# Weight-block sums of a two-layer trunk kernel: a fourth block formed in SBUF by adding transfers, and the others spread out

## What is computed

```python
for i in range(DEPTH):                       # DEPTH = 2
    mem_kv = rmsnorm(mem, mem_norm[i]) @ w_mem_kv[i]
    u = rmsnorm(h, norm_mix_pre[i])
    ...                                      # layer 0: Mamba-2 SSD, layer 1: windowed attention with sinks
    mixed = jnp.concatenate([y_mix, y_mem], axis=-1) @ w_out
    h = h + rmsnorm(mixed, norm_mix_post[i])
    f = squared_relu_mlp(rmsnorm(h, norm_mlp_pre[i]), w_up[i], w_down[i])
    h = h + rmsnorm(f, norm_mlp_post[i])

def squared_relu_mlp(u, w_up, w_down):
    return jnp.square(jax.nn.relu(u @ w_up)) @ w_down      # w_up 1024 x 4096, w_down 4096 x 1024
```

## Time and profile before

| what | value |
|---|---|
| runs, median of 3 | 1314.51 us (1312.38, 1314.51, 1319.97) |
| profiled execution | 1316.26 us, its span 1314.5 us |
| TensorE busy | 1288.1 us, 98% of the span |
| VectorE, ScalarE, GpSimd busy | 812.3, 657.4, 162.8 us |
| DMA | 230.01 MB, mean 175 GB/s |
| mean granted TensorE clock | 0.992 |
| chain that ended last | PE 87%, DMA 5%, DVE 4%, ACT 2%, issue 1% |

### The profile page before, as it was taken

The page is one execution under the profiler, slowest core; times in us unless marked ns, Lnnn a source line. Parts: engine busy times, 40 slices in busy tenths (PEclk is TensorE's granted clock), DMA queues, the critical chain, the costliest instruction groups (busy, mean ns, idle before and its releaser), DMA issues.

```text
span 1314.5 us, 17993 instructions
## 1 busy us (share of the span) xinstructions
PE 1288.1 (98%) x6743; PEld 1062.0 (81%) x6743; DVE 812.3 (62%) x1160; ACT 657.4 (50%) x1141; POOL 162.8 (12%) x195
## 2 busy tenths in 40 slices
PE   9999999999978999999999999999999999999998
PEld 8777788888757988888888888777779888888886
DVE  5586686887432733336787973776464334478887
ACT  6644455677332532325555743675453323365563
POOL 0046362551110000000000000000000000000000
PEclk9999999999989999999999999999999999999999
DMA  6378773343977269678656526656534775966654
GB/s 218 105 249 282 194 231 105 121 150 112 251 166 208 80 190 226 207 181 207 205 193 194 189 81 156 130 117 156 137 124 140 183 216 169 222 199 191 193 166 156
DMA packets 110367, 230.01 MB, mean 175 GB/s; under 512 B 8134, under 2 KB 18646, under 8 KB 110038
## 3 DMA queue, kind: packets, MB, share of 16 engines
q1 hardware_dynamic: 84240, 159.93, 36.9%
q0 software_dynamic: 21760, 67.11, 23.2%
q10 hardware_dynamic: 4294, 2.00, 0.9%
HBM read 225.69 MB, written 70.04 MB: 225 GB/s over the span
## 4 chain that ended last, share of the span: by engine, by line
PE 87%; DMA 5%; DVE 4%; ACT 2%; issue 1%; ACTq 0%; DVEq 0%; SPq 0%
PE G L1961 47%; PE G L2390 4%; PE G L2392 4%; PE G L2388 4%; DMA raw<-in_ssd_w_out 3%; PE X L2390 3%; PE X L2388 3%; PE X L2392 3%; PE X L1984 3%; PE X L2042 3%; PE G L2042 2%; PE X L2157 1%; DVE wlo L1275 1%; PE X L2231 1%; PE X L2148 1%
## 5 line engine op out<-in xcount | busy, mean ns | idle before, releaser
L1275 DVE TENSOR_TENSOR wlo<-raw,whi 128x1024 fp32r<-128x1024 f32 x143 | 175.7, 1229 | 297.4 <-ACT whi L693 297.3
L1961 PE MATMUL G<-uhi,whi 128*128 128x512 f32 x736 | 294.4, 400 | 1.0 <-DVE sz L1400 0.6
L1961 PE MATMUL G<-uhi,wlo 128*128 128x512 f32 x736 | 287.1, 390 | 0.0
L1961 PE MATMUL G<-ulo,whi 128*128 128x512 f32 x736 | 286.7, 390 | 0.0
L693 ACT ACTIVATE whi<-raw 128x1024 fp32r<-128x1024 f32 x143 | 151.5, 1059 | 257.5 <-PE G L1961 165.4
L1098 ACT ACTIVATE whi<-raw 128x1024 fp32r<-128x1024 f32 x112 | 118.7, 1059 | 122.0 <-PE G L2392 69.9
L1735 DVE TENSOR_TENSOR wlo<-raw,whi 128x1024 fp32r<-128x1024 f32 x112 | 136.4, 1223 | 65.4 <-ACT whi L1098 65.3
L1961 PEld LDWEIGHTS G<-uhi,whi 128*128 128x128 f32 x736 | 138.2, 188 | 32.3 <-issue 2.3
L1961 PEld LDWEIGHTS G<-uhi,wlo 128*128 128x128 f32 x736 | 138.1, 188 | 29.5 <-DVE wlo L1323 0.2
L1961 PEld LDWEIGHTS G<-ulo,whi 128*128 128x128 f32 x736 | 138.3, 188 | 28.6
L608 POOL DMA_DIRECT2D tsum<-in_w_down x32 | 32.7, 1022 | 559.4 <-PE G L1961 554.7
(11 more groups left out here) (371 smaller groups left out, 2483.3 us busy)
## 6 DMA issues: line engine op xcount, KB each, us to landing
tsum<-in_w_down POOLq DMA_DIRECT2D x48, 1024.0 KB, 10.1
raw<-in_w_up SPq DMA_DIRECT2D x64, 512.0 KB, 4.2
raw<-tsum SPq DMA_DIRECT2D x64, 512.0 KB, 3.8
raw<-in_w_down SPq DMA_DIRECT2D x48, 512.0 KB, 4.2
raw<-in_ssd_w_in SPq DMA_DIRECT2D x20, 512.0 KB, 3.7
raw<-in_w_mem_kv SPq DMA_DIRECT2D x16, 512.0 KB, 3.6
raw<-in_ssd_w_out SPq DMA_DIRECT2D x16, 512.0 KB, 6.3
raw<-in_swa_w_in SPq DMA_DIRECT2D x16, 512.0 KB, 4.3
```

Of the source, the lines that this page charges most:

```text
L1275: dve.tensor_tensor(wlo[q][:, :, :], raw[q % 2][:, :, :], whi[q][:, :, :].bitcast(F32), ALU.subtract).then_inc(lo_done, 1)
L1961: mm = pe.matmul(o, st, mv, start=(kt == 0 and fresh and not go_on), stop=(q == total - 1 and k == 1), skip_group_check=True)
```

## The change

**The fourth block.** `tsum` has three blocks. The 16 transfers per layer that were blocks 2 and 3 become the 8 of block 2. M6's eight panels are now loaded by SP from block 2 into the raw buffers, the same data as M1's. Behind each such load, GpSimd waits for its landing (`down_in`) and issues an accumulating transfer of the 512 KB panel of `w_down` onto the raw buffer in SBUF (`last_add`, landing counted by the new semaphores `full_in`). ACT's `right_hi` waits for `full_in` in M6 where it waited for `down_in`.

**The others.** The 16 copies of blocks 0 and 1 now begin with three at panels 2, 4 and 6 (`COPY_AT`), and the rest go two per SSD unit, which leaves room for three adds in units 6 and 7. The remaining 13 transfers for layer 0 wait for panels 54, 57, 60 and then for every second one from 72 to 90. For layer 1 there are 16, at every second panel from 162 to 174 and from 190 to 206.

**The boundary behind layer 0's MLP** (odd `m`) has another order on ACT and DVE, for token tiles 2 and 3.

```diff
-WEIGHT_SUM = {M2: (0, (5, 11)), M1: (2, (8, 14)), M7: (1, (6, 12)), M6: (3, (10, 16))}
-W0_SUM_AT = tuple(range(54, 64)) + tuple(range(72, 100, 2))
-W1_SUM_AT = tuple(range(162, 184, 2)) + tuple(range(190, 216, 2))
+WEIGHT_SUM = {M2: (0, (5, 9)), M1: (2, (8, 12)), M7: (1, (6, 10)), M6: (2, (8, 12))}
+COPY_AT = (2, 4, 6)
+W0_SUM_AT = (54, 57, 60) + tuple(range(72, 92, 2))
+W1_SUM_AT = tuple(range(162, 176, 2)) + tuple(range(190, 208, 2))
...
+            def last_add(i, q):
+
+                n = 8 * M6 + q
+                src = a["w_down"][i][2048:4096, 512:1024][256 * q:256 * q + 256, :].rearrange("(k p) n -> p k n", p=P)
+                ps.wait_ge(down_in[n % 4], 16 * (DOWN * i + n // 4) + 16)
+                ps.dma_start(down_raw[n % 4][:, :, :], src, accum_op=ALU.add).then_inc(full_in[n % 4], 16)
+
+            def first_copies(n):
+
+                weight_copy(n // 8, n // 4 % 2, n % 4, n // 4)
 
             ps.wait_ge(consts, 4)
+            for n, p in enumerate(COPY_AT):
+                ps.wait_ge(panel_done, p)
+                first_copies(n)
...
                 if v < 8:
-                    for r in range(2 * (v % 2), 2 * (v % 2) + 2):
-                        weight_copy(v // 4, v // 2 % 2, r, v // 2)
+                    for n in (2 * v + 3, 2 * v + 4):
+                        if n < 16:
+                            first_copies(n)
+                        else:
+                            weight_sum(0, n - 16)
...
             for i, at_panel in enumerate((W0_SUM_AT, W1_SUM_AT)):
-                for n in range(24):
-                    ps.wait_ge(panel_done, at_panel[n])
+                for n, p in enumerate(at_panel, 16 - len(at_panel)):
+                    ps.wait_ge(panel_done, p)
                     weight_sum(i, n)
+                for q in range(8):
+                    last_add(i, q)
...
@@ boundary on ACT @@
-                norm_out(m, 3)
+                if m % 2 == 0:
+                    norm_out(m, 3)
                 norm_in(m, 2)
                 hi(nb, 2)
+                if m % 2:
+                    norm_out(m, 3)
                 norm_in(m, 3)
...
@@ right_hi on ACT @@
-                    act.wait_ge(down_in[n % 4], 16 * (DOWN * i + n // 4) + 16)
+                    if n < 8 * M6:
+                        act.wait_ge(down_in[n % 4], 16 * (DOWN * i + n // 4) + 16)
+                    else:
+                        act.wait_ge(full_in[n % 4], 16 * (2 * i + (n - 8 * M6) // 4) + 16)
...
@@ boundary on DVE @@
-                lo(nb, 1)
                 if m % 2:
                     late_half(m // 2, 3)
-                gained(m, 3)
-                add_out(m, 3)
-                lo(nb, 2)
-                scaled(m, 2)
-                lo(nb, 3)
-                scaled(m, 3)
+                    lo(nb, 1)
+                    gained(m, 3)
+                    lo(nb, 2)
+                    scaled(m, 2)
+                    add_out(m, 3)
+                    lo(nb, 3)
+                    scaled(m, 3)
```

More of the change, by code:

```diff
@@ L398, in build @@
         sum_in = [sem(f"sum_in{r}") for r in range(4)]
+        full_in = [sem(f"full_in{i}") for i in range(4)]
         v2_done = sem("v2_done")
@@ L405, in build @@
         cs_rows = nc.dram_tensor("cs_rows", (UNITS, SR * P), F32, kind="Internal").ap()
-        tsum = [nc.dram_tensor(f"tsum{i}", (4, FF // 2, 512), F32, kind="Internal").ap() for i in range(2)]
+        tsum = [nc.dram_tensor(f"tsum{i}", (3, FF // 2, 512), F32, kind="Internal").ap() for i in range(2)]
         def product_ready(eng, i, r, t):
@@ L597, in weight_copy @@
                 rows = slice(512 * r, 512 * r + 512)
-                src = a["w_down"][i][0:2048, 0:512] if x < 2 else tsum[i][0 if x == 2 else 2]
+                src = a["w_down"][i][0:2048, 0:512] if x < 2 else tsum[i][0]
                 if done:
@@ L612, in weight_sum @@
                 x, r = divmod(n, 4)
-                done = 4 + 6 * i + x
+                done = 4 + 4 * i + x
                 if x == 0:
@@ L619, in weight_sum @@
                     weight_copy(i, 2, r, done)
-                elif x == 3:
+                else:
                     weight_add(i, 2, 0, 1, r, done)
[L622 to L625, removed]
+            def last_add(i, q):
[5 more added lines that the diff above has]
+                weight_copy(n // 8, n // 4 % 2, n % 4, n // 4)
             ps.wait_ge(consts, 4)
+            for n, p in enumerate(COPY_AT):
+                ps.wait_ge(panel_done, p)
+                first_copies(n)
             ps.wait_ge(bc_in, 48)
```

## The result

The changed kernel takes **1336.92 us** (median of 4, 1333.70 to 1337.89) beside 1314.05 us for the kernel before (median of 4). The ratio is 1.0162, with a 95% interval of 1.0126 to 1.0198. The forecast was 1307 us with a range up to 1318, so it is wrong in size and in sign. The profiled execution took 1337.89 us, the longest of the four, and its span is 1336.2 us.

What follows compares the result with a forecast made beforehand. TensorE, busy 1288.1 of 1314.5 us, was taken as the bound, leaving about 26 us idle plus clock loss to win. 1316.26 - 16.3 - 1.5 + 9.2 + 1.0 = 1308.7, forecast 1307 us as median, range 1300 to 1318.

Steps and rivals of the forecast that it cites:

- Output projection of layer 0: With fewer adds beside the load behind `h`, two TensorE stalls and their clock loss go: 16.3 us gained.
- rival of a late load: Layer 0's output projection: `h` and gain vectors hold the load until 359, only some 11 us gained, 1312.5 us; chance 0.15.
- Boundary behind layer 1's output projection: Without the copy of panel 180 beside a load, one short TensorE wait goes: 1.5 us gained, between 0 and 1.6.
- M6: Down products with adding loads: four-buffer loop no longer fits, 3.1 us plus 1.5 of clock per layer, 9.2 lost, bounds 1.7 and 27.
- L: Adding load's time from issue to landing in M6: taken as 5.5 us, bounded by 3.8 and 10.1.
- The loads beside it: Plain panel loads in M6's four-buffer loop, counted as 4.0 us each.
- rival of the loop as the bound: M6 panels 50 to 55: 2 us per layer for each us of add time; 1321 us from about 9; chance 0.15.
- Boundary behind layer 0's MLP: New order shortens two waits but adds one of 2.3 us at the fourth panel: 1 us lost, bounds -1 and +3.
- At nothing: Early copies at panels 2, 4, 6 and adds in units 6 and 7 at most 1 us each; up-product spacing nothing.
- The rival built on it, an add at the price of a load: M6: adding into SBUF costs little more than a load, 3.8 to 4.6 us; kernel some 1301 us; chance 0.2.

Runs made afterwards that it cites:

- run 10: Kernel before, all sums through DRAM, background transfers further apart: panels 54, 57, 60, then two apart, four apart in the down products; 1297.08 us, ratio 0.9863.
- run 6: Kernel before with the change's early copies alone (three at panels 2, 4 and 6, then two per unit); 1317.70 us, ratio 1.0010.
- run 7: Kernel before with the change's new ACT and DVE orders at the boundary behind the down products alone; 1319.48 us, ratio 1.0026.
- run 4: Changed kernel with each adding load cut to the first half of its panel, 256 KB in place of 512 KB; 1313.61 us.
- Run 5: Changed kernel with adding loads on two of M6's eight panels per layer, then those two as plain loads; 1314.75 and 1306.30 us.
- run 2: Changed kernel without the 16 adding loads, M6's last block being the third source block alone; 1300.17 us.
- run 3: Changed kernel with the 16 adding loads made plain ones that overwrite, same queue, bytes and waits; 1313.83 us.
- run 8: Kernel before with the wider spacing of adds and copies under the up products alone, all four blocks through DRAM; 1305.85 us, ratio 0.9904.
- run 9: Kernel before, all sums through DRAM, none issued between panels 60 and 72, last ones two panels apart beside the down products; 1304.07 us, ratio 0.9907.

## Why the prediction was wrong, point by point

- **Output projection of layer 0: right.** 16.3 us forecast, 16.3 measured between S and U. The load behind `h` landed in 8.7 us (forecast 9), and the clock stayed at 1.00 from 360 to 420 us. The rival of a late load is out.
- **Boundary behind layer 1's output projection: right in its cause, somewhat low.** 1.5 forecast (up to 1.6), 1.9 measured, also in run 10, with one of the two short waits gone. In runs 6 and 7, which keep the old transfers there, X0 to X1 took 207.5 and 207.3 us for 205.9, so the gain is 1.9 to 3.5.
- **M6: this step failed.** Forecast 4.6 us in each layer, measured 16.6 and 18.5, together 35 us where even the upper bound (at L = 10.1) was 27. So a wrong L isn't enough: by the forecast's own rule L = 8.4 makes 3.1 + 2 x 2.9 + 1.5 = 10.4 us in each layer. What failed is the sum of the loop's round. Three sizes in it were wrong. *L* was taken as 5.5, scaled down from the least disturbed 1 MB add into DRAM; it is 8.4, and 7.9 without a crowd. The scaling took off 3.4 us for the 512 KB less (8.8 to 5.4), and here 256 KB more already cost 3.2 (5.2 in run 4 to 8.4). The size 10.1 that bounded it from above belonged to an add of twice the bytes, into DRAM; that adding into SBUF would be nearer to it than to a plain load was in the range but not in the choice. *The loads beside it* were taken as 4.0 us; those on the chain took 6.0 to 6.7. *The issue* of 1.2 us stands on the chain once more in the second round, where two third-block loads land together and the second adding load waits for the issue of the first (750.54 and 751.83 us). It was not in the sum at all. The start was as forecast: the first load of the two rounds is issued at 726.39 us, where the forecast has 739.2, less the 12.9 by which U comes earlier. From there to the end of the last low part the forecast had 24.3 us (739.2 to 763.5), and the trace has 38.7 (726.39 to 765.06): 6.32 + 0.29 + 8.22 + 1.06 + 1.24 and small gaps, 17.2 us, for the first round and 21.5 for the second. That is 14.4 more than forecast, with the 3.1 that it had lost anyway 17.5, of which 16.6 are left at X0. The forecast let a round grow by L alone. From run 4 to the changed kernel L grows by 3.2 us and the loss by 9.7 and 11.6, three to three and a half per us of L and not two, and two things grow with it: the third-block loads on the chain took 4.3 to 5.7 us in run 4 and 6.0 to 6.7 in the changed kernel, and the mean granted clock in layer 0's M6 was 0.91 in run 4 (722 to 762 us) and 0.83 in the changed kernel (726 to 766 us). How much each has of the difference, no run separates.
- **The mechanism was named**, as the rival of the loop as the bound, with its place (ACT's high part waiting for the landed add, TensorE at the last panels of M6), but with a chance of 0.15 and 1321 us at L = 9. Against it I had held that "only eight panels" are concerned and the first two adds run early. Run 5 shows that two panels of eight are enough for 8 us. The mechanism is the rival's, its price of two us for each us of L is not.
- **Boundary behind layer 0's MLP: the wait right, the cost too low.** The wait of 2.2 us at the fourth panel (L2073) stands where the forecast had 2.3. But 1 us lost was forecast, bounds -1 and +3, and run 7's times say 3.4 (2.0 to 5.0), its stretches 1.0 to 2.9. Part of what was missed is the clock behind that wait (last section).
- **At nothing: too low for the early copies in some executions.** "At most 1" was 3.5 in the changed kernel's profiled execution, 1.3 by run 6's median (interval 0 to 2.6), and under 1 in the five profiled executions of runs 2 to 5. I had looked for waits of TensorE near by, not for what runs beside the load of 52.8 us. The adds in SSD units 6 and 7 and the spacing in the up products cost nothing that the stretches show.
- **The sum:** 1316.26 - 16.3 - 1.9 + 16.6 + 18.5 + 1.4 (U to X0 of run 2 over before) + 3.5 = 1338.1, measured 1337.89. These are the table's stretches put together again, and no proof of the parts.
- The price that the Trainium skill has for GpSimd's queue ("DMA: Bandwidth & Descriptors", section "Latency and other measured facts": a first byte 0.4 us later than from SP) fits this case only in direction. A plain load from GpSimd's queue took 5.0 us in run 5, where SP's loads of the third block around it took 3.8, as in the kernel before. How much of the 1.2 us is the first byte, no row here shows. The rival built on it, an add at the price of a load, is refuted by run 5 (7.9 us against 5.0) and by run 3 against the changed kernel (5.8 against 8.4).

## What to carry to other kernels

A load that waits for another load into the same buffer adds its whole latency to the loop. Here a round took 17.2 us where TensorE needs 10.9. Count load, issue, second load and both converting steps against the time in which the consumer eats all buffers, before counting bytes. When an operation isn't in the trace, take the dear end of its bounds where it sits in such a loop, or measure it alone first. And before a transfer is made to disappear, try to move it: in run 10 spacing the background transfers brought the whole gain of the two output projections, and none of the five stretches became longer. Count the spacing in time: two panels apart was 10.9 us in the up product and 5.4 in the down product.

## What was not expected of the hardware

- An adding load of 512 KB into SBUF took 7.9 us at the median with no other beside it, against 5.0 for the plain one from the same queue and 3.8 from SP's. Its issue held GpSimd for 1.20 us against 0.71, and it cost 1.5 us more of all sixteen DMA engines and 128 more packets.
- With such loads on them, the engines showed a share of 1.10 at 192 GB/s in one stretch; with plain ones 0.94 at 312. Stretches of the changed kernel with other loads among them had more, 261 at 1.10 from 742 to 750 us.
- The same early copies beside the same early load cost 0.3 to 0.8 us in five profiled executions and 3.5 and 3.7 in two, one of the changed kernel and one of run 6, with a longer wait for `sz` and a lower clock behind it. What makes the wait longer stays open.
- The clock behind one and the same short wait differed between executions. The kernel before took 323.2 us from U to X0, run 10, with the same orders of work and the same wait of 1.3 us at L2042, 321.7. Stretches at that wait (us, busy times, PEclk, DMA share, GB/s), before, then run 10:

```profile
774.00:782.00 8.00, 6.25 (x48) 5.78 (x48) 7.19 (x10) 4.65 (x9) 0.00 (x0) 0.79 0.42 133
```

```profile
755.00:763.00 8.00, 6.26 (x61) 5.79 (x61) 7.08 (x10) 6.30 (x13) 0.00 (x0) 1.00 0.47 136
```

TensorE is busy as long in both, with 48 matmuls at a clock of 0.79 and 61 at 1.00. The difference of 1.5 us is the clock. With the wait of 2.2 us that the new order has, the clock fell in run 2 (0.79) and in run 7 (0.82) as well, but in runs 3 and 4 it stayed at 1.00 behind the same wait. With the wait of 1.3 us it stayed at 1.00 in runs 6, 8 and 9 too, so the kernel before is the odd one of five.
